# The feed-forward stage of a two-block kernel: stored weight sum in a tile of its own, earlier first down loads, spread reloads, new orders at three places

## The reference, cut to what matters

```python
# first block
o = merged @ w_out
x = x + g1 * rms_norm(o, g_post_mix)
h2 = rms_norm(x, g_pre_ffn) * (1.0 + sc2) + sh2
f = jnp.square(jax.nn.relu(h2 @ w_ff1)) @ w_ff2
x = x + g2 * rms_norm(f, g_post_ffn)
...
# second block
x = x + mixed @ w_out
x = x + jnp.square(jax.nn.relu(rmsnorm(x, norm2_g) @ w_ff_up)) @ w_ff_down
return rmsnorm(x, norm_f_g)
```

## Time and profile before

| | |
|---|---|
| median of 3 runs | 3157.76 us (3156.78 to 3157.79) |
| the profiled execution, its own time | 3159.14 us |
| its span in the trace | 3157.3 us |
| PE busy | 2840.0 us (90%) |
| DVE busy | 1960.5 us (62%) |
| ACT busy | 1311.1 us (42%) |
| POOL busy | 63.5 us (2%) |
| mean granted PE clock | 0.951 |
| transfer queue q1 | 468.44 MB, 43.6% of 16 engines' span |

### The profile page before, as it was taken

How to read it: one execution, slowest core, us unless ns; L and a number is a source line. 1 busy time by engine, 2 the same in 40 slices (tenths; PEclk the granted TensorE clock), 3 DMA queues, 4 the chain that set the end, 5 groups by cost and what they waited for, 6 DMA issues and landing times. The chain is left out here.

```text
span 3157.3 us, 44344 instructions
## 1 busy us (share of the span) xinstructions
PE 2840.0 (90%) x17980; PEld 2234.6 (71%) x17980; DVE 1960.5 (62%) x2923; ACT 1311.1 (42%) x1914; POOL 63.5 (2%) x143
## 2 busy tenths in 40 slices
PE   6999848799999897979999989997798999989798
PEld 3766724477788676857778788886677888868676
DVE  6669887565766454674877524655636476645476
ACT  3026945457655332443451113231323465533244
POOL 0000010000000000000000001110000000000000
PEclk8999879899999999989999999997799999999999
DMA  6420100235666766821454331105214556666684
GB/s 239 167 80 27 34 0 1 87 107 179 214 227 227 279 207 225 287 100 57 134 144 117 118 124 50 67 33 163 91 54 145 194 200 239 224 257 203 203 306 160
DMA packets 200074, 471.25 MB, mean 149 GB/s; under 512 B 31360, under 2 KB 60160, under 8 KB 193280
## 3 DMA queue, kind: packets, MB, share of 16 engines
q1 hardware_dynamic: 199872, 468.44, 43.6%
HBM read 344.09 MB, written 124.29 MB: 148 GB/s over the span
## 5 line engine op out<-in xcount | busy, mean ns | idle before, releaser
L2025 PE MATMUL psum<-merged_operand 128*128 128x512 f32 x1536 | 371.7, 398 | 28.0 <-DVE merged_operand L2471 19.4
L2025 PEld LDWEIGHTS psum<-merged_operand 128*128 128x128 f32 x1536 | 293.3, 192 | 97.5 <-DVE merged_operand L2471 28.8
L2025 PE MATMUL psum<-h_half_operand 128*128 128x512 f32 x1344 | 326.6, 400 | 35.7 <-DVE h_half_operand L2471 35.5
L2025 PEld LDWEIGHTS psum<-h_half_operand 128*128 128x128 f32 x1344 | 256.9, 192 | 98.7 <-DVE h_half_operand L2471 42.1
L2025 PE MATMUL psum<-h_half_operand,weight_parts_operand 128*128 128x512 f32 x768 | 182.3, 398 | 12.5 <-DVE weight_parts_operand L2471 6.3
L2025 PEld LDWEIGHTS psum<-h_half_operand,weight_parts_operand 128*128 128x128 f32 x768 | 146.5, 192 | 47.3 <-ACT stage L2219 8.3
L3417 PE MATMUL psum<-h_high,weight_high 128*128 128x512 f32 x480 | 152.7, 399 | 12.5 <-DVE h_low L243 12.5
L230 DVE CAST weight_high<-weight_ring 128x1024 fp32r<-128x1024 f32 (+1 forms) x64 | 37.9, 592 | 199.3 <-PE psum L3417 103.8
L3417 PE MATMUL psum<-h_low,weight_high 128*128 128x512 f32 x480 | 149.0, 392 | 0.0
L3417 PE MATMUL psum<-h_high,weight_low 128*128 128x512 f32 x480 | 148.5, 391 | 0.0
L2471 DVE TENSOR_TENSOR weight_parts_operand<-weight_ring,weight_parts_operand 128x1024 fp32r<-128x1024 f32 x66 | 80.8, 1224 | 101.2 <-ACT weight_parts_operand L2173 100.8
(11 more groups left out here) (593 smaller groups left out, 6033.1 us busy)
## 6 DMA issues: line engine op xcount, KB each, us to landing
o<-in_w_ff SPq DMA_DIRECT2D x80, 512.0 KB, 6.3
merged<-hidden_terms SPq DMA_DIRECT2D x56, 512.0 KB, 5.7
hidden_upper<-in_w_ff_down SPq DMA_DIRECT2D x48, 512.0 KB, 5.2
weight_ring<-in_w_out SPq DMA_DIRECT2D x32, 512.0 KB, 3.5
hidden_terms<-weight_parts SPq DMA_DIRECT2D x16, 1024.0 KB, 3.9
hidden_terms<-weight_ring SPq DMA_DIRECT2D x16, 1024.0 KB, 3.9
hidden_upper<-in_w_ff_up SPq DMA_DIRECT2D x32, 512.0 KB, 6.4
o<-hidden_terms SPq DMA_DIRECT2D x28, 512.0 KB, 5.7
```

What stands on the lines that cost most here:

```text
L2025: mm = pe.matmul(bank, w[:, at:at + P], tiles(r, i), start=opens and m == 0, stop=closes and m == 2, skip_group_check=resumed)
```

## The change

(a) In `p65` steps the tiles of `w_raw` change places: the three loads go to tiles 0, 1 and 2, s1 is made in tile 2 and s2 in tile 3, which no p65 load writes. `load_w` of a p65 step no longer waits for the store. Instead DVE waits, before it writes s2, for the store of three steps ago. `load_w` of the steps 32 to 34 keeps its wait for the store.

(b) SP issues the loads of down step 0 with pair 14 and those of step 1 at the start of pair 15 (`h_raw[0]` and `h_raw[1]` change places for that), those of step 2 before the last record's store; ACT and DVE round and split step 0 a little earlier in pair 15.

(c) The reload of x (`x_kept`, 4096 KB in one transfer ahead of step 0) becomes eight transfers of 512 KB, issued with steps 2 to 9; the first use by DVE in the second call goes from n = 9 to n = 11. The first slabs of the stage after the first call are issued at n = 50 to 53 instead of n = 8.

(d) Behind the output products, the weights of early iteration 1 (slab MIX + 1) are rounded and split ahead of the last h tiles; in the loops over m `square_h11` and `keep_p1` stand ahead of the roots, squares and shifts, which start one iteration later; `shift_h` of the first half goes to m = 0 and 1, scales and shifts of the second half all to m = 9 (second call: m = 4).

(e) At the end of the first call, the `X3_1` squares are added up on POOL and not on DVE; the squares go through four tiles instead of two; PE takes the sum of `X3_1` after that of `Y_0E`.

(f) ACT's table for the logarithm is loaded at n = 50, one step ahead of the root at n = 51.

Squares, buffers and a helper:

```diff
-        SQUARES = [("PE", KT), ("DVE", KT), ("DVE", OUTS), ("DVE", OUTS), ("DVE", OUTS), ("DVE", KT), ("PE", OUTS), ("PE", KT)]
+        SQUARES = [("PE", KT), ("DVE", KT), ("DVE", OUTS), ("DVE", OUTS), ("DVE", OUTS), ("POOL", KT), ("PE", OUTS), ("PE", KT)]
...
-        sq_down = flat_r[:, 4 * HALF:6 * HALF]
+        sq_down = [tiles(flat_r, 4), tiles(flat_r, 5), tiles(parts, 5), tiles(parts, 6)]
+        acc_pool = tiles(parts, 7)
...
-        h_raw = [flat_h[:, 12 * HALF:14 * HALF], flat_h[:, 14 * HALF:16 * HALF], flat_r[:, 0:2 * HALF], flat_r[:, 2 * HALF:4 * HALF]]
+        h_raw = [flat_h[:, 14 * HALF:16 * HALF], flat_h[:, 12 * HALF:14 * HALF], flat_r[:, 0:2 * HALF], flat_r[:, 2 * HALF:4 * HALF]]
...
-            return tiles(sq_down, j % 2)
+            return sq_down[j % 4]
...
+        def down_weights(n):
+            at = 2 * HALF if steps[n][0] == "p65" else 0
+            return w_raw[n % 3][:, at:at + 2 * HALF]
+
```

SP, `load_w`, `load_h`, `store_s2`, the loop over the pairs and that over the steps:

```diff
-                        if steps[n - 3][0] == "p65":
+                        if steps[n - 3][0] == "p65" and what != "p65":
...
-                        sp.dma_start(tiles(to, 0), w_down[24 + u // 2][:, at]).then_inc(sem, 16)
+                        sp.dma_start(tiles(to, 1), w_down[24 + u // 2][:, at]).then_inc(sem, 16)
...
-                        sp.dma_start(tiles(to, 1), w_down[u // 2][:, at]).then_inc(sem, 16)
+                        sp.dma_start(tiles(to, 0), w_down[u // 2][:, at]).then_inc(sem, 16)
...
-                        wait_product(sp, "p5", PAIRS - 2)
-                    elif n == 1:
...
+                    elif n == 1:
+                        wait_product(sp, "p5", PAIRS - 2)
...
-                    sp.dma_start(s2_dram[k], tiles(w_raw[n % 3], 1)).then_inc(s2_stored[k % 3].sem, 16)
+                    sp.dma_start(s2_dram[k], tiles(w_raw[n % 3], 3)).then_inc(s2_stored[k % 3].sem, 16)
...
-                    load_h11(i)
...
-                        load_w(0)
-                        load_h(0)
...
-                        load_w(2)
+                    load_h11(i)
+                    if i == PAIRS - 2:
+                        load_w(0)
+                        load_h(0)
...
-                store_record(PAIRS - 1)
+                load_w(2)
...
+                store_record(PAIRS - 1)
...
-                sp.dma_start(x[:], x_kept).then_inc(K.load_done.sem, 16)
...
-                    if n == 8 and after is not None:
-                        first_slabs(sp, K, *after)
+                    if 2 <= n < 2 + KT:
+                        sp.dma_start(x[:, n - 2, :], x_kept[:, n - 2, :]).then_inc(K.load_done.sem, 16)
+                    if 50 <= n < 50 + RING and after is not None:
+                        slab, cols = n - 50, after[1]
+                        sp.dma_start(K.ring[:, slab, 0:cols], after[0][slab]).then_inc(K.slab_loaded[slab].sem, 16)
```

PE, the loop over m and the end:

```diff
-                    if m == 1:
-                        sum_given(1)
-                    if first and m == 7:
+                    if first and m == 8:
...
+                    if m == 1:
+                        sum_given(1)
...
-                if first:
-                    sum_acc(5, acc_down, 2 * KT + 3 * OUTS)
-                sum_of(6, acc_early[:], ends=False)
+                sum_of(6, acc_early, ends=False)
...
+                    wait(pe, pool_added, KT)
+                    sum_of(5, acc_pool).then_inc(summed.sem, 1)
```

ACT, `square`, the output products' end, the loop over m, pair 15, the steps:

```diff
-                    if j >= 2:
-                        wait_taken(act, j - 2)
+                    deep = 2 if first and j < begin[Y_0A] else 4
+                    if j >= deep:
+                        wait_taken(act, j - deep)
...
+                round_w(MIX + 1)
...
-                    if m < PAIRS:
+                    if 0 < m < PAIRS:
...
-                    if m == 1:
+                        square_h11(m - 2)
+                    if m < PAIRS:
+                        keep_p1(m)
+                    if m == 2:
...
-                    if first and m in (0, 6):
+                    if first and m in (0, 1):
...
-                            shift_h(0, k + (OUTS if m else 0))
-                    if first and m == 7:
+                            shift_h(0, k + OUTS * m)
+                    if first and m == 8:
...
-                    if first and m in (8, 9):
-                        for k in range(OUTS):
-                            shift_h(1, k + OUTS * (m - 8))
-                    if m >= 2:
-                        square_h11(m - 2)
-                    if m < PAIRS:
-                        keep_p1(m)
+                    if first and m == 9:
+                        for k in range(KT):
+                            shift_h(1, k)
...
+                    else:
+                        round_down_w(0)
+                        round_down_h(0)
...
-                    if i == PAIRS - 1:
-                        round_down_w(0)
-                        round_down_h(0)
...
+                    if n == 50:
+                        load_log_table(3)
```

POOL, new:

```diff
+            if first:
+                @block.gpsimd
+                def _(pool):
+                    for t in range(KT):
+                        j = begin[X3_1] + t
+                        wait(pool, sq_made, j + 1)
+                        if t == 0:
+                            pool.tensor_copy(acc_pool, sq_at(j)).then_inc(pool_added.sem, 1)
+                        else:
+                            wait(pool, pool_added, t)
+                            pool.tensor_tensor(out=acc_pool, in0=acc_pool, in1=sq_at(j), op=ALU.add).then_inc(pool_added.sem, 1)
+
```

DVE, `add_down_weights`, the same places as on ACT, the steps:

```diff
-                        dve.tensor_tensor(out=tiles(raw, 0), in0=tiles(raw, 0), in1=tiles(raw, 2), op=ALU.add).then_inc(w_added.sem, 1)
+                        dve.tensor_tensor(out=tiles(raw, 2), in0=tiles(raw, 1), in1=tiles(raw, 2), op=ALU.add).then_inc(w_added.sem, 1)
...
-                        dve.tensor_tensor(out=tiles(raw, 1), in0=tiles(raw, 0), in1=tiles(raw, 1), op=ALU.add).then_inc(w_added.sem, 1)
+                        if k >= 3:
+                            wait(dve, s2_stored[k % 3], 16 * (k // 3))
+                        dve.tensor_tensor(out=tiles(raw, 3), in0=tiles(raw, 2), in1=tiles(raw, 0), op=ALU.add).then_inc(w_added.sem, 1)
...
+                    if k == 4:
+                        rest_of_w(MIX + 1)
...
+                    rest_of_w(MIX + 1)
...
-                    if first and 2 <= m < 6:
-                        for t in (2 * (m - 2), 2 * (m - 2) + 1):
-                            add_scaled(1, t, hid_b[:, 2 * t + 1, :], 16, KT + t, tmp_up, root_o_up)
...
+                            add_scaled(1, t, hid_b[:, 2 * t + 1, :], 16, KT + t, tmp_up, root_o_up)
+                    if first and 4 <= m < 8:
+                        for t in (2 * (m - 4), 2 * (m - 4) + 1):
...
-                    if m == 8:
+                    if m == (9 if first else 4):
...
-                    if m in (8, 9):
-                        for k in range(OUTS):
-                            scale_h(1, OUTS * (m - 8) + k)
+                        for k in range(KT):
+                            scale_h(1, k)
...
+                    else:
+                        rest_of_down(0)
...
-                    if i == PAIRS - 1:
-                        rest_of_down(0)
...
-                        for t in {51: (), 52: (), 53: (0,), 54: (1, 2), 55: (3, 4, 5, 6, 7)}[n]:
-                            if t == 0:
-                                wait(dve, summed, 4)
-                            add_square(X3_1, t, acc_down, t == 0)
```

59 lines of the change are left out of this document (30 added, 29 removed).

## The result

The changed kernel takes **3067.51 us** (median of four runs, 3066.41 to 3073.16), against 3157.78 us before on the same chip: ratio 0.9715, 95% interval 0.9698 to 0.9731, 90.3 us less. The prediction was 3071 us, with a gain of 86.7. The profiled execution after took 3068.56 us, with a span of 3066.8, 90.5 us shorter than that of the earlier trace rows.

The account below looks back on a forecast made before the run. PE bounds the kernel wherever it is fed; in p65 steps the s2 store's latency on SP sets the pace. Terms 51.8 + 21.5 + 5.5 + 1.0 + 5.0 + 1.9 = 86.7 us less give 3071 us; range 3055 to 3090.

Parts of the forecast that it names:

- (a): p65 steps of both calls: without the store's wait on SP, 51.8 us gained, with 3 us per call still lost.
- DMA share near 0.95: p65 steps in the profile after: the transfers' busy share was to be near 0.95, with PE steps of 5.5 us.
- (b), (c): Start of the down products, both calls: earlier first loads and x reloaded in eight parts gain 10.5 and 11.0, together 21.5 us.
- The 2.90 us ahead of step 0: PE's wait for the last hidden tile's ReLU at the first down step: stays, costing 4.5 us with slow matmuls behind it.
- (d): Early up products: the new order gains 5.5 us in the first call and 1.0 in the second.
- (e), first call: End of the first call: four square tiles and no adds on DVE, less POOL's blocking of DVE, gain 5.0 us.
- The 9.7 us that it started from: End of the first call: how much earlier DVE would go on, at 1389.8, before POOL's blocking is counted.
- (e), second call: End of the second call: the last square could start at about 3142.7 instead of 3144.58, gaining 1.9 us.
- Transfers as the bound: Rival: transfers bound the p65 steps; at 6.2 us a step the time is 3088 us; chance 0.14.
- POOL blocking to the full: Rival: POOL blocks DVE fully at the first call's end, gain there 0 instead of 5, 3076 us; chance 0.12.
- The wait moving to DVE: Rival: in p65 steps the store's wait only moves to DVE's second add; with no gain there, 3123 us; chance 0.04.
- slower: Rival: the same DVE wait beats all gains, p65 steps growing from 7.7 to more than 8.8 us; chance 0.01.

Follow-up runs that it names:

- experiments 1 and 2: 1: changed kernel, p65 loads again waiting on SP for the s2 store, 3125.76 us; 2: kernel before, only s2's own tile and no such wait, 3098.49 us.
- experiment 3: The changed kernel with x loaded back in one transfer of 4096 KB ahead of step 0: 3088.41 us.
- experiment 4: The changed kernel with the first down steps' loads and step 0's split in their old order, the reload of x still in eight parts: 3067.36 us.
- Experiment 5: The changed kernel with the old order of the early up products on PE, ACT and DVE in both calls: 3073.95 us.
- experiment 6: The changed kernel with the first call's seven adds and one copy of the X3_1 squares on DVE instead of POOL: 3062.77 us.
- experiments 6 and 7: 6: the changed kernel with POOL's adds on DVE, 3062.77 us; 7: the changed kernel with eight more POOL adds that nothing reads, 3069.16 us.
- experiment 8: The changed kernel with two tiles of squares instead of four and no logarithm table loaded ahead: 3067.38 us.

## Why the prediction was right

- **(a)** The mechanism held: SP's round through one store's latency was the pace (experiments 1 and 2), and PE's own 5.467 us is the next limit. The size was off by 7.1: "I take a remaining loss of 3 us per call, as the share is so high" was the wrong step. That loss is 0.0, and the 13 steps of the earlier trace rows did not hold some 1 us that steps further back lost too. The share of 0.68 before was read as 5.3 us of work per step, that is, divided by the 13 steps that PE did in this window. But 220 GB/s over 100.66 us are 84 tiles, 14.1 steps of six: 4.9 us each. After, 91 tiles in 87.47 us at 0.86 are 15.2 steps at 5.0 us. The work per tile is the same before and after, 0.81 and 0.83 us of share; the estimate was too high because SP was moving more steps' tiles than PE worked off there. "DMA share near 0.95" was wrong for the same reason.
- **(b), (c)** 22.4 for 21.5. The 4096 KB held step 3 (experiment 3). The prediction named the causes in the right order, and the part of the earlier hidden terms is small: 0.2 and 2.4 us (experiment 4). The 2.90 us ahead of step 0 stayed in both calls as said. What they cost is not one number: 29.45 - 24.6 = 4.9 in the first call, 27.82 - 24.6 = 3.2 in the second, where step 0 happened to run at full speed. The prediction took 4.5 in both, so 1.3 us of the second call's 12.3 are luck.
- **(d)** 5.6 for 5.5, and 1.0. Experiment 5 gives the old stretch back exactly. The walk through both lists gave the period of 7.2 us (PE's starts at 743.40 and 750.63 are 7.23 apart). The parts fit less well than their sum. Of the two waits of 2.6 and 1.7 us that the prediction put at the start there is one, of 3.93 us, with 12 slow matmuls behind it:

```profile
708.38 4.61 PE L2033 MATMUL psum<-h_half_operand,weight_parts_operand 128*128 128x512 f32 x12 [3.93 <-ACT stage L2228]
```

  Counted from the start of the stretch, PE has done three products about 2.1 us earlier than before (after 14.5 us instead of 16.6), where 3.7 were forecast; it gains another 4.0 in the loop, where 3.0 were, and loses 0.5 behind it, where 1.2 were. That these add up to nearly the forecast is luck.
- **(e), first call** 3.6 for 5.0. From the end of PE's last product (1335.5) to DVE's next block are 10.0 us, predicted "about 10 us instead of 15.4"; and PE's last step is 2.13 late, as the term allowed for.

```profile
1345.49 0.75 DVE L2522 SCALAR_TENSOR_TENSOR merged<-late_terms,mod,weight_parts 128x512 f32<-128x512 f32 x1 [5.43 <-issue]
```

  That this came near is luck in part, because both halves of the term were off. The 9.7 us that it started from were too many: it put 5.7 us between PE's last product and DVE's block, and experiment 6 shows 8.7 there without any work on POOL (1333.26 to 1341.98). Behind the last product ACT has four squares of the result in PSUM to make, until 1335.77, where the sum counted one. All in all the end of the call is 7.3 us shorter there than before (53.38 to 46.08). Of that, POOL's meetings with DVE took 3.7 (experiments 6 and 7), more than the adds cost on DVE. The four tiles are only 0.9 of the gain (experiment 8).
- **(e), second call** 0.3 for 1.9: the step that failed is "the last square, now at 3144.58, could start at about 3142.7: 1.9". The square did move by 1.9, but PE's ten sums were as late as it, and end the call.
- **The rivals.** Transfers as the bound: fell, six tiles leave room, eight do not. POOL blocking to the full: fell as a price for the whole part (0 instead of 5.0; measured 3.6), right as a mechanism. The wait moving to DVE, and slower: fell, DVE waits for ACT alone in the 16 steps shown.

## What to carry to other kernels

A wait for a store ahead of a load, on a queue that issues everything in order, sets the pace for all that stands behind it; look for the transfer in the chain that ended last, and give the store a tile of its own. A busy share of the transfer engines is to be divided by the tiles that moved in its window (GB/s times its length), and not by the steps that PE did there; and add load before you believe that the transfers are full. Work moved to POOL to relieve DVE can cost DVE more than the work did, if DVE has operations of two SBUF inputs at that time; count how often the two would meet. What a change of order gives is read from the stretch that it touches, and when one wait is removed, the engine that was nearly as late (PE's sums, step 3's weights) sets the next one.
